# Mixer products over half the array's rows or columns, given in turn to its two halves; alr and dt from one product; operands without zero halves

## What is computed

```python
def hybrid_mixer(h, ...):
    proj = h @ w_in
    q, k, v, g, alr, z, xs, bm, cm, dt = jnp.split(proj, IN_SPLITS, axis=-1)
    # 256, 256, 512, 512, 16, 512, 512, 128, 128 and 8 columns
    log_a = jax.nn.log_sigmoid(alr @ gla_a_w + gla_a_b) / GLA_TAU
    o = gla_chunked(q, k, v, log_a)             # 4 heads, 64 keys, 128 values, chunks of 64
    o = rmsnorm(o, gla_norm_w) * silu(g)
    xs, bm, cm = split(silu(causal_depthwise_conv(concat([xs, bm, cm]), conv_w, conv_b)))
    dt = jax.nn.softplus(dt + dt_bias)
    y = ssd_chunked(xs, dt, -exp(a_log), bm, cm)  # 8 heads of 64, 2 groups of state 64, chunks of 128
    y = rmsnorm((y + d_skip * xs) * silu(z), ssd_norm_w)
    return concat([o, y]) @ w_out

def gla_chunked(q, k, v, log_a):
    b = cumsum(log_a)                            # within a chunk of 64
    qe, ke = q * exp(b), k * exp(-b)
    att = where(causal, qe @ ke.T, 0)
    k_tail = k * exp(b_last - b)
    contrib = k_tail.T @ v                       # per chunk
    s_prev = inter_chunk_states(exp(b_last), contrib)
    return att @ v + qe @ s_prev
```

## Time and profile before

| | us |
|---|---|
| median of 3 runs | 2529.87 (2528.81 to 2530.36) |
| time of the profiled execution | 2529.46 |
| its span | 2527.7 |
| PE busy | 2324.4 (92%) |
| DVE busy | 1662.2 (66%) |
| ACT busy | 918.3 (36%) |

### The profile page before, as it was taken

The page is one execution under the profiler, slowest core; times in us unless marked ns, Lnnn a source line. Parts: engine busy times, 40 slices in busy tenths (PEclk is TensorE's granted clock), DMA queues, the critical chain, the costliest instruction groups (busy, mean ns, idle before and its releaser), DMA issues.

```text
span 2527.7 us, 31543 instructions
## 1 busy us (share of the span) xinstructions
PE 2324.4 (92%) x11714; PEld 1639.0 (65%) x11714; DVE 1662.2 (66%) x2928; ACT 918.3 (36%) x1372; POOL 746.4 (30%) x610
## 2 busy tenths in 40 slices
PE   5999999998999999999999989998898998877777
PEld 4789999687776677777766666677774544322222
DVE  6867895765654655655555545447578888787875
ACT  2234443414543444444444431013423433232332
POOL 0000000001565565566556400000023443433331
PEclk9999999898999999999999989999899999999999
DMA  9555877454999999999999963036489999999996
GB/s 371 204 230 203 333 272 277 182 202 151 370 420 421 419 420 421 419 413 421 420 411 421 401 224 133 34 112 243 162 330 358 416 421 420 421 421 422 420 421 290
DMA packets 108768, 824.54 MB, mean 326 GB/s; under 512 B 11896, under 2 KB 14200, under 8 KB 15360
## 3 DMA queue, kind: packets, MB, share of 16 engines
q0 software_dynamic: 83520, 608.21, 58.3%
q1 hardware_dynamic: 24368, 211.99, 21.7%
q10 hardware_dynamic: 720, 2.25, 0.3%
HBM read 821.35 MB, written 1.05 MB: 325 GB/s over the span
## 4 chain that ended last, share of the span: by engine, by line
PE 68%; DMA 14%; DVE 10%; issue 5%; ACT 2%; POOL 1%; SPq 0%; DVEq 0%; ACTq 0%; POOLq 0%
PE ps L768 9%; PE ps L770 9%; PE ps L769 9%; DMA ring<-in_uv,arena 8%; PE ps L754 8%; PE ps L1145 7%; PE ps L832 6%; PE ps L1638 4%; DMA arena<-in_uv,arena 4%; PE ps L787 4%; PE ps L1179 3%; DMA ring<-in_moe_w_down,arena 2%; PE ps L762 2%; PE ps L992 1%; PE ps L1004 1%
## 5 line engine op out<-in xcount | busy, mean ns | idle before, releaser
L1996 DVE TENSOR_TENSOR ring_r<-ring,arena_r 128x2048 fp32r<-128x2048 f32 x168 | 385.1, 2292 | 73.0 <-ACT arena_r L2444 68.8
L2444 ACT ACTIVATE arena_r<-ring 128x2048 fp32r<-128x2048 f32 x210 | 402.5, 1917 | 57.4 <-DMA ring<-in_moe_w_down,arena 16.4
L1638 PE MATMUL ps<-ring,sel 128*128 128x512 f32 x568 | 271.0, 609 | 66.3 <-ACT sel L2444 65.9
L2960 POOL DMA_INDIRECT ring<-in_uv,arena x142 | 133.2, 938 | 591.8 <-DVE arena L2264 347.6
L2444 ACT ACTIVATE arena<-ps 128x256 f32<-128x256 f32 (+2 forms) x236 | 107.9, 457 | 434.6 <-PE ps L770 106.6
L1638 PE MATMUL ps<-arena,sel 128*128 128x512 f32 x456 | 221.2, 614 | 48.5 <-ACT sel L2444 47.5
L2444 ACT ACTIVATE sel<-cs,arena 128x128 f32<-128x128 f32 x256 | 102.8, 401 | 412.4 <-DVE arena L2395 327.0
L768 PE MATMUL ps<-arena_r 128*128 128x512 f32 (+1 forms) x672 | 242.6, 361 | 4.1 <-DVE ring_r L1996 4.1
L1638 PEld LDWEIGHTS ps<-ring,sel 128*128 128x128 f32 x568 | 100.7, 190 | 215.7 <-ACT sel L2444 133.2
L2944 POOL DMA_INDIRECT ring<-in_moe_w_gate,arena x108 | 161.0, 1491 | 160.5 <-PE ps L770 99.7
L2417 DVE CUSTOM_DVE_ANT_0 accb<-ring,ps 128x1024 f32<-128x1024 f32 x142 | 173.4, 1221 | 47.9 <-DMA ring<-in_uv,arena 44.6
(11 more groups left out here) (319 smaller groups left out, 4336.9 us busy)
## 6 DMA issues: line engine op xcount, KB each, us to landing
ring<-in_ada_w SPq DMA_DIRECT2D x24, 1024.0 KB, 10.1
ring<-in_ada_w SPq DMA_DIRECT2D x12, 2048.0 KB, 8.1
ring<-in_w_in SPq DMA_DIRECT2D x10, 2048.0 KB, 12.8
ring<-in_w_ada SPq DMA_DIRECT2D x8, 2048.0 KB, 7.8
ring<-in_ffn_w_gate SPq DMA_DIRECT2D x14, 1024.0 KB, 6.4
ring<-in_ffn_w_up SPq DMA_DIRECT2D x14, 1024.0 KB, 7.0
ring<-in_ffn_w_down SPq DMA_DIRECT2D x14, 1024.0 KB, 7.5
ring<-in_w_out SPq DMA_DIRECT2D x6, 2048.0 KB, 10.5
```

What stands on the lines that cost most here:

```text
L1638: last = e.matmul(ps.banks[2 * t + c], m.diag[:, i % NDIAG, :], rows[:, 1024 + 512 * c:1536 + 512 * c], start=(i % 128 == 0), stop=(i % 12 ...
L1996: v(e.tensor_tensor(ring_low[ring.half[unit]], ring.buf[unit], mo.high[unit_at[unit] % NHIGH].bitcast(F32), ALU.subtract), ("low", unit))
L2444: A.mark(e.activation(out, src, func, **kw), name)
L2960: e.indirect_dma_start(base, None, T["uv"], bass.IndirectOffsetOnAxis(m.index[t][:, n:n + 1], 0)).then_inc(row_sems[ROWS[i][0]], 16)
```

## The change

`alr` and `dt` come out of one product: the tile "rest" gets 72 columns behind the 256 of bm and cm, namely dt (8), 24 zeros, alr (16), 16 zeros and dt again (8). Its result has dt in partitions 0 to 7 and 64 to 71, and alr in 32 to 47. The small operations on dt and cum run over 72 partitions and so hold both copies. `cb` then takes its heads in turn from partitions 0 to 7 and 64 to 71, each into its own bank. `att`, `gm`, `state` and the state part of `o` contract over 64 partitions only, and the two matmuls of a pair, one on partitions 0 to 63 and one on 64 to 127, follow each other and write different banks. `ke`, `kt` and the unpadded bm take the place of `kep`, `ktp` and `bpad`, and `spad` is no longer cleared. `y` has the same matmuls in another order.

```diff
-                tile = cols_of(("w_in", l, "rest"), 280)
-                b = bank(("alr", l))
-                P.mark(summed_as(b[0:16, 0:256], [(tile[:, k, 264:280], hT[:, k, :]) for k in range(8)],
-                                 ("hT", "norm1", l)), ("alr", l))
-                b = bank(("dt", l))
-                P.mark(summed(b[0:8, 0:256], [(tile[:, k, 256:264], hT[:, k, :]) for k in range(8)]), ("dt", l))
+                tile = cols_of(("w_in", l, "rest"), 328)
+                b = bank(("alr dt", l))
+                P.mark(summed_as(b[0:72, 0:256], [(tile[:, k, 256:328], hT[:, k, :]) for k in range(8)],
+                                 ("hT", "norm1", l)), ("alr dt", l))
...
-                for p in range(4):
-                    b = bank(("cb", l, p))
+                for p in (0, 2):
+                    bs = [bank(("cb", l, p + i)) for i in range(2)]
                     for j in range(2):
-                        h = 2 * p + j
-                        last = e.matmul(half(b, j), selb[0:8, 128 * h:128 * h + 128], m.cum[0:8, :],
-                                        start=True, stop=True)
+                        for i, b in enumerate(bs):
+                            h, r = 2 * (p + i) + j, slice(64 * i, 64 * i + 8)
+                            last = e.matmul(half(b, j), selb[r, 128 * h:128 * h + 128], m.cum[r, :],
                                             start=True, stop=True)
...
+                        for o, r in enumerate(rows64):
+                            last = e.matmul(bs[o][:, at:at + 128], m.ke[r, c, s], m.qe[r, c, s],
+                                            start=True, stop=True)
...
+                    for g, r in enumerate(rows64):
+                        last = e.matmul(bs[g][:, s], m.xc[r, 4, s], m.xc[r, 5, s], start=True, stop=True)
...
+                for ns in ((0, 1), (2,)):
                     for c in range(2):
+                        for n in ns:
+                            r = rows64[n % 2]
+                            last = e.matmul(half(bs[n], c), m.kt[r, n // 2, 128 * c:128 * c + 128],
+                                            m.v_tm[r, n // 2, 256 * c:256 * c + 256], start=True, stop=True)
...
-                for h in range(4):
-                    b = bank(("o", l, h))
+                for c in range(2):
+                    heads = [(2 * c + o, bank(("o", l, 2 * c + o)), r) for o, r in enumerate(rows64)]
                     for t in range(2):
                         s = slice(128 * t, 128 * t + 128)
+                        for h, b, r in heads:
+                            e.matmul(b[:, s], m.v_tm[:, t, 128 * h:128 * h + 128], m.attm[:, h, t, :],
+                                     start=True, stop=False)
                         for n in range(max(1, 2 * t), 2 * t + 2):
+                            for h, b, r in heads:
+                                last = e.matmul(b[:, 64 * n:64 * n + 64], m.spad[r, h, n - 1, :],
+                                                m.qe[r, c, 64 * n:64 * n + 64], start=False, stop=(n == 2 * t + 1))
...
-                for h in range(4):
-                    r = slice(64 * (h % 2), 64 * (h % 2) + 64)
-                    v(e.tensor_tensor(m.kep[r, h, :], b[r, h // 2, :], m.lm[r, h // 2, :], ALU.mult), ("kep", l))
+                v(e.tensor_tensor(m.ke, b, m.lm, ALU.mult), ("ke", l))
...
-                for n in range(4):
-                    r = slice(64 * (n % 2), 64 * (n % 2) + 64)
-                    v(e.tensor_copy(m.ktp[r, n, :], b[r, 256 * (n // 2):256 * (n // 2) + 256]), ("ktp", l))
+                v(e.tensor_copy(m.kt, v4(taken(("ktail", l)), 2)), ("kt", l))
...
-                for z in (m.xbc[:, :, 0:3], m.kep, m.bpad, m.gm, m.ktp, m.attm, m.spad):
+                for z in (m.xbc[:, :, 0:3], m.gm, m.attm):
```

More of the change, by code:

```diff
@@ L291, in program @@
         ps = Psum([psum[:, 512 * i:512 * i + 512] for i in range(8)])
-        in_pv, in_x, in_ones, in_cs, in_wide, in_sel, in_ms = [(sem(f"{n}_loaded"), 16) for n in
-                                                      ("pv", "x", "ones", "cs", "wide", "sel", "ms")]
+        in_pv, in_x, in_ones, in_cs, in_wide, in_sel, in_ms = [(sem(f"{n}_loaded"), 16 * k) for n, k in
+            (("pv", 1), ("x", 1), ("ones", 1), ("cs", 1), ("wide", 1), ("sel", 2), ("ms", 1))]
         row_sems = [sem(f"rows{i}_gathered") for i in range(NROWS)]
@@ L631, in sp @@
                         e.dma_start(ms, T["ms"]).then_inc(in_ms[0], 16)
-                        e.dma_start(selb[0:8, :], T["sel"]).then_inc(in_sel[0], 16)
+                        for at in (0, 64):
+                            e.dma_start(selb[at:at + 8, :], T["sel"]).then_inc(in_sel[0], 16)
                     load_ada(hidden.pop(0))
@@ L860, in mixer @@
                 for c in range(2):
-                    last = e.matmul(half(b, c), pvc(f"gla_a_w{l}", 128 * c, 128, rows=16), m.alr[0:16, :],
+                    last = e.matmul(half(b, c), pvc(f"gla_a_w{l}", 128 * c, 128)[32:48, :], m.alr[32:48, :],
                                     start=True, stop=True)
@@ L902, in mixer @@
                 done(("w_in", l, "v"))
-                b = bank(("gm", l))
-                e.wait_ge(*V["bpad", l])
+                bs = [bank(("gm", l, g)) for g in range(2)]
                 e.wait_ge(*A["xc bc", l])
[L906 to L910, removed]
+                for t in range(2):
+                    s = slice(128 * t, 128 * t + 128)
+                    for g, r in enumerate(rows64):
+                        last = e.matmul(bs[g][:, s], m.xc[r, 4, s], m.xc[r, 5, s], start=True, stop=True)
+                        if t:
+                            P.mark(last, ("gm", l, g))
                 e.wait_ge(*A["xc", l])
@@ L1774, in mixer @@
                     conv(k)
-                e.wait_ge(*A["xc bc", l])
-                for g in range(2):
-                    r = slice(64 * g, 64 * g + 64)
-                    v(e.tensor_copy(m.bpad[r, g, :], m.xc[r, 4, :]), ("bpad", l))
                 some(hidden, 3)
@@ L3055 @@
         vec(f"conv_b{l}", x["conv_b"][l])
[L3056 to L3057 removed]
+        for at in (0, 64):
+            rows(f"dt_bias{l}", x["dt_bias"][l][:, None], at)
+            rows(f"a_log{l}", x["a_log"][l][:, None], at)
         vec(f"d_skip{l}", np.repeat(x["d_skip"][l], 64))
         vec(f"ssd_norm_w{l}", x["ssd_norm_w"][l])
[L3060 removed]
+        rows(f"gla_a_w{l}", x["gla_a_w"][l], 32)
     vec("final_w", x["final_norm_w"])
```

98 lines of the change are left out of this document (45 added, 53 removed).

## The result

| | before | after |
|---|---|---|
| median of the runs, us | 2530.11 (2528.81 to 2531.63, 4 runs) | 2513.22 (2511.71 to 2514.45, 4 runs) |
| profiled execution, us | 2529.46 | 2513.70 |
| its span, us | 2527.7 | 2511.9 |

The ratio is 0.9931, with a 95% interval from 0.9919 to 0.9943: 17.5 us less by it, between 14.4 and 20.5, and 16.9 by the medians. Against the 19.2 us of the sum, 2510.2 was forecast for the profiled execution.

What follows compares the result with a forecast made beforehand. PE was taken to bound both mixers; savings of 8.95 us in layer 0 and 10.28 in layer 1, 19.2 in all, took the profiled 2529.46 to 2510.2. Forecast median 2510.5, own range 2507 to 2513, 8-in-10 range 2504.5 to 2517.

Steps and rivals of the forecast that it cites:

- What bounds, and one to one: Both mixers: PE bounds them, and time it saves there comes off the whole kernel one to one.
- Merge (3.45 a layer): Start of each mixer: dt's 16 instructions go, saving 3.45 us a layer; the wider weight load costs nothing.
- low end: Rival, on alr: the half clock ends sooner, 2.8 us more saved per mixer, down to 2505; chance 0.05.
- `cb`, `att`, `gm`, `state`: Mixer products: pairing half-height calls brings layer 0's times to 1.93, 1.08, 0.64 and 1.93 us.
- Loads in single file: Rival, att, gm and o: weight loads do not pair, 2.6 us lost per mixer, 2516; chance 0.08.
- no pairs at these depths: Rival, the paired mixer products: none pair, only the merged dt counts, 2 x 3.45 us, 2523; chance 0.06.
- Both leftovers are one entry and one exit, so I take 0.10 a change: Full/half height changes: 0.10 us each from leftovers 0.19 and 0.20; eight in o cost 0.80, leaving o 0.53 shorter.
- bounds of 0 and 0.3: Cost per height change in o: at 0, o takes 3.1 us; at 0.3 us each, 5.5.
- I take that as the likelier case: Behind cb in both mixers: the clock stays full, as after osum's 1.8 us of one-column products.
- the clock still falls: Rival, behind cb: half clock costs 1.65 us in layer 0, up to 3.3 in layer 1; 2514 to 2515.5; chance 0.17.
- `y` (forecast 0): End of each mixer: the same matmuls and columns as before, so 0 us gained.
- The late ada tile: DVE in layer 0's mixer: waits 2.6 us for this tile, nearly all covered; cost 0.1, ignored.

Runs made afterwards that it cites:

- experiments 1 and 2: Unedited reruns: the changed kernel twice more, 2515.3 and 2513.76 us; the kernel before once more, 2531.78 us.
- merge_only: Kernel before, with only alr and dt merged into one product of 72 columns, padded operands kept: 2522.39 us, ratio 0.9968 to the kernel before.
- o_full: Changed kernel with o back at full height, head by head, state padded with zeros: 2515.29 us, ratio 0.9938 to the kernel before.
- experiment 9: Kernel before, with cb reading all 128 rows, zeros in the unused ones, nothing paired: 2525.16 us, ratio 0.9977 to the kernel before.
- experiment 5: Changed kernel with o's full-height calls first, then its half-height calls, two height changes instead of eight: 2513.32 us, with start flags mended 2513.3 us.
- experiment 8: Changed kernel with cb reading all 64 rows of its half: 2512.15 us; second kernel, also with o's full-height calls first: 2511.25 us.
- blocks: Changed kernel with half-height calls in blocks, all of one half then the other, in cb, att, gm, state, o and y: 2529.09 us, ratio 0.9995 to before.
- cb_one_half: Changed kernel with all 16 cb calls reading partitions 0 to 7, order over banks kept: 2521.78 us, ratio 0.9959 to the kernel before.

## Why the prediction was right, and where its sizes were off

**What bounds, and one to one.** Right. PE stays without a gap from `alr dt` to `g`; the two mixers are 16.9 us shorter by the means of their traces, where 19.2 was forecast, and the whole kernel 16.9 by the medians. That the two figures are the same is chance: at the first gather it was 18.5, and experiments 1 and 2 show intervals behind it that move by 4.4 and by 3.5 us under an unchanged program.

**Merge (3.45 a layer).** Right, and alone worth 2523 as its rival said. A bonus was not in the sum: `alr dt` takes 5.84 and 5.05 where `alr` took 6.30 and 5.62. That goes towards the "low end" rival, but `merge_only` took 6.65, `o_full` 6.18, and `alr` alone in the second trace of before 5.32, so it is scatter for the most part. The half clock that the forecast reads into these products is in layer 1's row: 0.50 from 447 to 451 us, while they start 0.427 us apart. For layer 0 the row says 1.00, but the starts are 0.427 apart there too, until 41.2 us; the trace's first record of the clock is at 41.6.

**`cb`, `att`, `gm`, `state`.** 1.89, 1.09, 0.65 and 1.93 against 1.93, 1.08, 0.64 and 1.93. The pace of pairs, taken from a stage 1,600 us later with calls up to twice as wide, carried over to 8 rows and to 128 columns. "Loads in single file" and "no pairs at these depths" are out. But these figures hold the step into half height only; the step out stands in the group behind, and no term had it: 0.15 us behind `gm`, 0.20 behind `state`, 0.15 in `ktail` (0.59 for the 0.44 of experiment 9, where all is at full height).

**`o` and the change of height: the term that was mis-sized.** "Both leftovers are one entry and one exit, so I take 0.10 a change" is the step that failed. A change lengthens two intervals between starts, the one across the border and the next: at the start of `z`, where PE comes back to full height, they are 0.303 and 0.320 us in place of 0.216. The 0.20 of the earlier trace rows, reckoned from start to start, holds the later part of the entry and the earlier part of the exit, and the 0.19 of the earlier trace rows, reckoned from end to end, one whole entry. So a change costs 0.15 to 0.2 beside wide calls as well as among short ones, nearly double. In the chain of after, the groups of `o` show 0.20 into full height (0.64 - 4 x 0.11) and 0.15 into half (0.37 - 2 x 0.11), and experiment 5 gives 0.17 over six. Eight changes are then 1.36 and not 0.80: `o` is 4.38 for 4.40 before, where 0.53 less was forecast, and the whole of that term is lost in each mixer. This lay well inside the bounds of 0 and 0.3. The Trainium skill (TensorEngine Tiling (Array Packing), Tiling Modes) says that a change of tiling mode drains TensorE; the trace agrees in that each change costs time.

**The clock.** "I take that as the likelier case" held in layer 0 of the first trace only. Over the six traces of kernels with 8-row `cb` in turns it fell in layer 1 six times and in layer 0 twice. In the first trace it cost `att` 0.16, `ktail` 0.46 and `val` 1.01 over layer 0, 1.6 in all. So the rival "the clock still falls" came true by half, near its price of 1.65 in total; it had half of that in `att`, and the clock fell later. The nearest row that I had picked, `osum` with its one-column products over 128 rows, was the wrong likeness: those are as short as `cb`'s but deep. Experiments 8 and 9 show that depth was a thing to compare, though not the only one (see Open).

**`y` (forecast 0).** From the first call to `w_out` it takes 2.82 us in layer 0 of after, where it took 3.10; 0.28 gained that I had not looked for (0.13 in layer 1).

**DVE.** The late ada tile costs 1.54 on DVE, not 2.6, and nothing on PE, as forecast. (The wider tile brings 48 columns more, 192 KB and not 224; this changes nothing.)

**How near the sums came, and by what luck.** From `alr` to `w_out` layer 0's mixer is 9.04 us shorter, for 8.95 forecast. That is two errors against each other: `o` and the unpriced steps back to full height took 0.9 (by the chain 0.41 in `o`; 0.15, 0.20 and 0.14 behind `gm`, `state` and `o`), and things outside the sum gave 1.0 (`alr dt` 0.46, `bc` 0.19, `y` 0.28, the transposes before `cb` 0.06). Layer 1's is 9.01 shorter for 10.28: the same 0.9 is missing and 1.4 by the clock (against the terms, `att` 0.17, `ktail` 0.20 and `val` 1.01), and `alr dt`, `bc`, `y` and the transposes gave 0.95 back.

**Open.** In `blocks`, `cb` was just as shallow, took 2.01 and 2.20 us, and the clock stayed at 1.00 behind it in both layers; it fell later, in `o`. So few rows are not sufficient. They are not necessary either: the calls of `o`, behind which it fell in both layers, are 64 and 128 rows deep. I have no run that tells what else counts. Nor is it tried whether a wait or another product between `cb` and `att` would do as well as depth.

## What to carry to other kernels

Half-height products in turn run at the pace of pairs even where they are 8 deep or 128 wide, but each change of height costs 0.15 to 0.2 us, into half height and back: count the changes first, and group the half-height calls (1.02 us for six changes fewer, where eight had eaten all that the pairs saved). When pricing such a step from a trace, take in the groups on both sides, and never compare an interval between starts with one between ends. Before you pair or shorten a stretch of shallow products, look at the granted clock behind it: here zeros in unused rows alone, at no loss of pace, gave back a third of what the whole rewrite did. Check a term by its own rows in the trace, since a median of a 2.5 ms kernel does not resolve 2 us.

## What the runs showed of the hardware that was not expected

- Calls of the two halves need not stand next to each other: blocks of two took as long as turns (`gm` 0.65, `state` 1.93, `cb` 2.01 us), blocks of four (`att`) 1.61 for 1.10. In these blocks the instructions start in another order than the list's.
- A step from calls of 8 rows to calls of 64 costs as much as a change of height: by the chain `att` takes 1.09 us behind `cb` over 8 rows, and 0.89 behind `cb` over 64 (second kernel of experiment 8).
- 16 products of 256 columns over 8 rows at full height of the tile took 3.56 us and over 128 rows 3.65; in two halves over 8 rows 1.89 and over 64 rows 1.93, all by the chain. Rows are free in time within 0.1 us, and not neutral for the clock: behind 8 rows at once in one half it fell in every trace (before, twice; merge_only; cb_one_half), behind 128 rows in none of two places.
- A second start flag in a bank reaches further than the columns of its own call: with it the sums of `o` came out incomplete, and with the flag on the bank's first call alone complete. Which columns are lost was not read out.
